# Normed input of four stages in buffers of its own, at 72, 68, 80 and 88 bytes past the weights' place

## Chip, cores and metric

The kernel runs on one core of a Trainium2 chip. The metric is the device time of one execution, in microseconds. The time before is 1128.12 us, the median of 3 runs (1127.64 to 1128.2).

## The reference

One sequence of 256 tokens with 1024 channels goes through a first block (a hybrid mixer with a state-space branch and three attention branches, and a gated feed-forward), and a second block of two layers: an HGRN2 mixer and a feed-forward, then a recurrent RG-LRU mixer and a feed-forward. All is float32. Cut to what the change touches:

```python
h = rmsnorm(x, norm_ffn[l])                     # first feed-forward
x = x + swiglu(h, w_ffn_gate[l], w_ffn_up[l], w_ffn_down[l])
...
for l in range(DEPTH_2):                        # second block, two layers
    hn = rmsnorm_2(x, norm_mix[l])
    if l % N_MIXERS == 0:
        mix = hgrn2_mixer(hn, ...)              # the "second mixer": hn @ w_in, w_in 1024 x 4096
    else:
        mix = rglru_mixer(hn, ...)              # the "third mixer"
    x = x + mix
    x = x + swiglu_2(rmsnorm_2(x, norm_ffn[l]), ffn_w_in[l], ffn_w_out[l])

def swiglu_2(h, w_in, w_out):
    gate, up = jnp.split(h @ w_in, [D_FF_2], axis=-1)   # D_FF_2 = 2816
    return (jax.nn.silu(gate) * up) @ w_out
```

## The kernel before

The normed input `h` is held transposed, channels on the 128 partitions, as 8 slices of 256 tokens. Each float32 value is split in two numbers of the type float32r, a high and a low part: `hh` and `hl` for the input, `whi` and `wlo` for the weights. A product of input and weights is then three: whi with hh, wlo with hh, whi with hl.

Weights come in units of at most 2048 elements per partition (1 MB) into a ring of three slots: `raw` by DMA, `whi` by ScalarE's copy (L1041), `wlo` by VectorE's or GpSimd's subtraction (L1465, L2143). The order of units is one list. All engines follow it, and each program is written out in order, with semaphores between engines.

TensorE has two forms of product. In `still` (L521, L524, L529) a 128 x 128 piece of the weights is loaded and the input moves, 256 columns at a time; gate and up units of a feed-forward and the column units of the mixers use it. A unit of 256 weight columns is 2 column blocks by 8 slices by 3 products, 48 matmuls, in groups of four slices. In `moving` (L541, L545, L549) a piece of the input is loaded and 512 columns of weights move; the token units (`hv`, `hg` of the second mixer) and the down and output products (`add_product`) use it.

The stages have a number e: 0 is the first mixer's input, 2 the first feed-forward, 3 the second mixer, 5 the second feed-forward, 6 the third mixer, 7 the third feed-forward. In each of them the normed rows `hn` are transposed on TensorE (L591), ScalarE copies the result into the high part (L1073) and VectorE subtracts for the low part (L1531). Each feed-forward has 11 gate and 11 up units, then 11 down units.

Every stage writes the same `hh` and `hl`. Their place matters for this change, so it is told in bytes of a partition. Buffers are laid out in the order in which they are written down, `raw` from 0. `whi` begins at 24,576 and `wlo` at 49,152; a slot is 8192 bytes and a piece of weights starts at a multiple of 512 bytes (in a unit of 256 columns). In this document "at n bytes" means n bytes past a multiple of 512, the weights' place:

| buffer | where it begins | at |
|---|---|---|
| hh, hl | 90,144 and 98,336 | 32 |
| eh, el (mixer outputs; share the space of hh, hl) | 90,112 and 98,304 | 0 |
| bh, bl (branch outputs, first mixer) | 133,696 and 141,888 | 64 |
| gh, gl (feed-forward's inner values) | 117,248 and 139,776 | 0 |
| gw (gate weights, third mixer) | 192,512 | 0 |

`sr`, 640 elements per feed-forward, is scratch in which GpSimd combines inner values for three of the down units (L2273 to L2277); ScalarE (L1284) and VectorE (L1888) round it.

Of the kernel before, what the change touches and what calls it, by code (L numbers as in the profile page):

```python
# [8 lines left out]
f32 = mybir.dt.float32  # L9
f32r = mybir.dt.float32r  # L10
# [11 lines left out]
SEVEN = (1, 4, 6)  # L22
# [53 lines left out]
def build(nc, a):  # L76
    V, A, G, T, S = nc.vector, nc.scalar, nc.gpsimd, nc.tensor, nc.sync
    vq, aq, gq, tq, sq = Waits(V), Waits(A), Waits(G), Waits(T), Waits(S)
    with ExitStack() as root:
# [3 lines left out]
        def sbuf(ctx, name, shape, dt=f32):  # L83
            return ctx.enter_context(nc.sbuf_tensor(name, shape, dt))
# [43 lines left out]
        dv = sbuf(mix, "dv", [128, 2, 128])  # L128
        mix.close()

        ffn = []
        for f in range(3):
            ctx = ExitStack()
            ffn.append((sbuf(ctx, f"gh_{f}", [128, 22, 256], f32r), sbuf(ctx, f"gl_{f}", [128, 22, 256], f32r),
                        sbuf(ctx, f"sg_{f}", [128, 2, 512]), sbuf(ctx, f"bc_f{f}", [128, 256]),
                        sbuf(ctx, f"sh_{f}", [128, len(SEVEN), 512], f32r), sbuf(ctx, f"sl_{f}", [128, len(SEVEN), 512], f32r),
                        sbuf(ctx, f"sr_{f}", [128, 640])))
            ctx.close()

        hg = ExitStack()  # L140
# [10 lines left out]
        nw = sbuf(hg, "nw", [128, 128])  # L151
        mstat = sbuf(hg, "mstat", [128, 16])
        bc_hg = sbuf(hg, "bc_hg", [128, 256])
        hg.close()

        lr = ExitStack()
# [8 lines left out]
        th = sbuf(lr, "th", [128, 8, 256])  # L165
        yg = sbuf(lr, "yg", [128, 8, 256])
        bc_lr = sbuf(lr, "bc_lr", [128, 256])
        gw = sbuf(lr, "gw", [128, 2, 4, 512])
        lr.close()

        def two(ap):
            return ap.rearrange("p (k t) -> p k t", k=2)
# [122 lines left out]
        NU = len(units)  # L295

        seven = {unit_at["down", f, n]: len(SEVEN) * f + i for f in range(3) for i, n in enumerate(SEVEN)}
        sums_raw, sums_hi, sums_lo = (t.rearrange("p (q n) -> p q n", n=512) for t in (
            hn_flat, eh[:, :, :].rearrange("p c t -> p (c t)"), el[:, :, :].rearrange("p c t -> p (c t)")))  # L300
# [86 lines left out]
        def bank_of(*key):  # L387
            return banks[turns[key][0]]
# [113 lines left out]
        def tensor_program():  # L502
# [49 lines left out]
            def of_norm(e):  # L552
                return (lambda k: hh_set(e, k)), (lambda k: hl_set(e, k))

            def project_columns(key, e, between=None):
                j = unit_at[key]
                b = turn(("col", *key), next_bank())
                tq.wait_ge(*free(("col", *key)))
                for m in range(units[j][2] // 128):
                    t = still(banks[b][:, 256 * m:256 * m + 256], j, m, hh, hl, range(8), *of_norm(e))  # L560
                    if between is not None and m == 0:
                        between()
                t.then_inc(s_full[b], 1)
                used[j, 0] = used[j, 1] = full("col", *key)

            def project_tokens(key, e, between=None):
                bs = [turn(("tok", *key, 0), next_bank()), turn(("tok", *key, 1), next_bank(), 2)]
                for part in range(2):
                    j = unit_at[(*key, part)]
                    for t in range(2):  # L570
                        if part == 0:
                            tq.wait_ge(*free(("tok", *key, t)))
                        tok = moving(banks[bs[t]][:, :], j, t, hh, hl, range(4 * part, 4 * part + 4), 0, 512, *of_norm(e),
                                     first=part == 0, last=part == 1)
                        if t == 1 or part == 1:
                            tok.then_inc(s_full[bs[t]], 1)
                    b, _, n = turns["tok", *key, 1]
                    used[j, 0] = used[j, 1] = (s_full[b], n - 1 + part)
                    if between is not None:
                        between(part)  # L580
# [21 lines left out]
            def project_pair(keys, e):  # L602
                js = [unit_at[key] for key in keys]
                bs = [turn(("col", *key), next_bank(), 2) for key in keys]
                for part in range(2):
                    for i, j in enumerate(js):
                        for m in range(2):
                            if part == 0:
                                tq.wait_ge(*free(("col", *keys[i])))
                            tok = still(banks[bs[i]][:, 256 * m:256 * m + 256], j, m, hh, hl, range(4 * part, 4 * part + 4),  # L610
                                        *of_norm(e), i0=4 * part, first=part == m == 0, last=part == m == 1,
                                        inside=(lambda: spread_factors(e)) if part == i == 1 and m == 0 and e == 3 else None)
                        tok.then_inc(s_full[bs[i]], 1)
                        used[j, part] = (s_full[bs[i]], turns["col", *keys[i]][2] - 1 + part)
                        if part == i == 0:
                            transposes(1, e)
                        if part == 1 and i == 0 and e != 3:
                            spread_factors(e)
# [411 lines left out]
        def scalar_program():  # L1030
# [38 lines left out]
            def turned(c, e):  # L1069
                for n in range(2):  # L1070
                    q = 2 * c + n
                    aq.wait_ge(*full("tr", e, q))
                    A.activation(hh[:, 2 * q:2 * q + 2, :], two(bank_of("tr", e, q)[:, :]), ACT.Copy).then_inc(s_hh, 1)  # L1073

            def project_pair(keys, e, bc, evacs):
                j = unit_at[keys[0]]
# [198 lines left out]
            add_product(("wo",), 4, 2)  # L1275

            def feed_forward(f, e, e2, again=None):
                gh, gl, sg, bc, sh, _, sr = ffn[f]

                def combined(j):  # L1280
                    if j in SEVEN:
# [169 lines left out]
        def vector_program():  # L1451
# [74 lines left out]
            def turned(c, e):  # L1526
                for n in range(2):
                    q = 2 * c + n
                    sl = slice(2 * q, 2 * q + 2)
                    vq.wait_ge(*hh_set(e, 2 * q))  # L1530
                    V.tensor_tensor(hl[:, sl, :], two(bank_of("tr", e, q)[:, :]), hh[:, sl, :].bitcast(f32),  # L1531
                                    ALU.subtract).then_inc(evacuated("tr", e, q), 1)

            def spread_factor(e):
# [344 lines left out]
            series = [None]  # L1879

            def feed_forward(f, e, e2, again=None):
                gh, gl, sg, bc, sh, sl, sr = ffn[f]

                def combined(j):
                    if j in SEVEN:
# [243 lines left out]
        def gpsimd_program():  # L2129
# [136 lines left out]

            def combine(f, j):

                q, inner, sr = seven[unit_at["down", f, j]], two(ffn[f][2][:, j % 2, :]), ffn[f][6]
                gq.wait_ge(*evac("col", "u", f, j))  # L2270
                if q > 0:
                    gq.wait_ge(s_comb_lo, q)
                d = own_p.mark(G.tensor_tensor(sr[:, 0:256], inner[:, 0, :], inner[:, 1, :], ALU.subtract))  # L2273
                G.tensor_tensor(sr[:, 384:512], inner[:, 0, 0:128], inner[:, 0, 128:256], ALU.subtract)
                gq.wait_ge(*d)
                G.tensor_tensor(sr[:, 256:384], sr[:, 128:256], inner[:, 0, 0:128], ALU.subtract)
                G.tensor_tensor(sr[:, 512:640], sr[:, 128:256], sr[:, 0:128], ALU.subtract).then_inc(s_comb, 1)  # L2277
# [144 lines left out]
```

## Time and profile before

| what | us |
|---|---|
| median of 3 runs | 1128.12 |
| the profiled execution | 1127.9 |
| its span, first to last instruction | 1126.6 |
| TensorE busy (matmuls) | 1111.4 |
| TensorE busy (weight loads) | 1034.5 |
| VectorE busy | 757.1 |
| ScalarE busy | 589.2 |
| GpSimd busy | 249.3 |

The granted clock of TensorE was 0.999 of the full 2.4 GHz over the span. PE is TensorE's matmul, PEld its weight load, DVE VectorE, ACT ScalarE, POOL GpSimd. Matmuls overlap, so a mean duration in a row is longer than the distance between two starts. In the timeline, like instructions that follow one another are merged into one row; its time is the start of the first of them. The names behind the arrow are the moving operand and then the loaded one: `hh,whi` is the input moving over loaded weights, `whi,hh` the weights moving over loaded input.

### The profile page before, as it was taken

How to read it: one execution, taken by the hardware profiler on the slowest of the kernel's cores; microseconds unless marked ns; L12 is line 12 of the kernel's file. 1: busy time of each engine (PE TensorE's matmuls, PEld its weight loads, DVE VectorE, ACT ScalarE, POOL GpSimd, SP SyncE). 2: the span in 40 equal slices, each digit the busy share in tenths (PEclk: the TensorE clock that was granted, in tenths of full speed). 3: DMA queues.
4: the chain of work that ended last, by engine and by line, in shares of the span. 5: the costliest groups of instructions: out<-in, count | busy, mean ns of one | idle time of the engine just before them, and what ended most of it. 6: DMA issues, size and time to landing. Idle time of an engine off the chain costs nothing.

```text
span 1126.6 us, 19386 instructions
## 1 busy us (share of the span) xinstructions
PE 1111.4 (99%) x8058; PEld 1034.5 (92%) x8058; DVE 757.1 (67%) x1160; ACT 589.2 (52%) x893; POOL 249.3 (22%) x202
## 2 busy tenths in 40 slices
PE   8999999999999999999999999999999999999997
PEld 7899989999989999888998889999889989999986
DVE  6755655677777456968897576444868896544676
ACT  6645555555545554536642554444536855444542
POOL 3022100000005554001411206553000003555100
PEclk9999999999999999999999999999999999999999
DMA  8689475544646756664545447656655355666561
GB/s 277 196 253 336 137 234 157 157 151 148 199 160 203 206 160 215 209 202 127 170 129 172 128 149 258 219 182 201 207 187 178 104 170 159 214 189 189 170 220 38
DMA packets 155090, 207.26 MB, mean 184 GB/s; under 512 B 9472, under 2 KB 128410, under 8 KB 155003
## 3 DMA queue, kind: packets, MB, share of 16 engines
q1 hardware_dynamic: 151274, 193.11, 54.6%
q0 software_dynamic: 3728, 12.92, 3.5%
q8 instruction: 64, 1.05, 0.4%
q14 instruction: 24, 0.19, 0.1%
HBM read 204.78 MB, written 4.24 MB: 186 GB/s over the span
## 4 chain that ended last, share of the span: by engine, by line
PE 81%; DVE 13%; ACT 4%; issue 2%; DMA 0%; POOL 0%; SPq 0%; DVEq 0%; ACTq 0%
PE bank L521 16%; PE bank L524 16%; PE bank L529 16%; PE bank L549 7%; PE bank L545 7%; PE bank L541 7%; DVE wlo L1465 4%; PE bank L660 1%; PE bank L656 1%; PE bank L659 1%; PE bank L946 1%; ACT whi L1041 1%; PE bank L860 1%; PE bank L870 1%; DVE area L1659 1%
## 5 line engine op out<-in xcount | busy, mean ns | idle before, releaser
L1465 DVE TENSOR_TENSOR wlo<-raw,whi 128x1024 fp32r<-128x1024 f32 x302 | 360.5, 1226 | 148.1 <-ACT whi L1041 147.1
L1041 ACT ACTIVATE whi<-raw 128x1024 fp32r<-128x1024 f32 (+1 forms) x362 | 356.5, 1034 | 80.5 <-PE bank L549 52.2
L521 PE MATMUL bank<-hh,whi 128*128 128x256 f32 x1784 | 284.6, 281 | 0.3 <-ACT hh L1073 0.3
L529 PE MATMUL bank<-hl,whi 128*128 128x256 f32 x1784 | 281.7, 279 | 0.4 <-DVE hl L1531 0.3
L524 PE MATMUL bank<-hh,wlo 128*128 128x256 f32 x1784 | 281.3, 279 | 0.0
L521 PEld LDWEIGHTS bank<-hh,whi 128*128 128x128 f32 x1784 | 240.7, 188 | 2.8 <-issue 2.0
L529 PEld LDWEIGHTS bank<-hl,whi 128*128 128x128 f32 x1784 | 239.9, 188 | 0.8 <-DVE hl L1531 0.8
L524 PEld LDWEIGHTS bank<-hh,wlo 128*128 128x128 f32 x1784 | 239.8, 188 | 0.0
L2143 POOL TENSOR_TENSOR wlo<-raw,whi 128x1024 fp32r<-128x1024 f32 x60 | 153.4, 2557 | 143.2 <-ACT whi L1041 143.1
L2150 POOL TENSOR_TENSOR st<-st,half 128x1 f32<-128x1 f32 x18 | 10.8, 607 | 476.1 <-DVE st L1524 442.1
L1288 ACT ACTIVATE sg<-sg 128x512 f32<-128x512 f32 x33 | 20.9, 633 | 96.4 <-DVE sg L1554 96.4
L1292 ACT ACTIVATE gh<-sg 128x512 fp32r<-128x512 f32 x33 | 20.8, 632 | 78.4 <-DVE sg L1901 78.4
L541 PE MATMUL bank<-whi,gh 128*128 128x512 f32 x192 | 59.3, 390 | 0.0
L545 PE MATMUL bank<-wlo,gh 128*128 128x512 f32 x192 | 59.2, 389 | 0.0
L549 PE MATMUL bank<-whi,gl 128*128 128x512 f32 x192 | 59.2, 389 | 0.0
L1901 DVE TENSOR_TENSOR sg<-sg,bank 128x512 f32<-128x512 f32 x33 | 22.7, 687 | 42.8 <-PE bank L529 40.7
L1554 DVE TENSOR_TENSOR sg<-bank,bc_f 128x512 f32<-128x512 f32 x33 | 22.7, 689 | 38.7 <-PE bank L529 38.7
L1066 ACT ACTIVATE bank<-x_sb 128x512 f32<-128x512 f32 x26 | 15.6, 600 | 61.9 <-DVE x_sb L1580 34.1
L1903 DVE TENSOR_TENSOR gl<-sg,gh 128x512 fp32r<-128x512 f32 x33 | 31.5, 956 | 23.3 <-ACT gh L1292 23.3
L549 PEld LDWEIGHTS bank<-whi,gl 128*128 128x128 f32 x192 | 36.0, 188 | 7.6
L545 PEld LDWEIGHTS bank<-wlo,gh 128*128 128x128 f32 x192 | 36.0, 188 | 7.5
L541 PEld LDWEIGHTS bank<-whi,gh 128*128 128x128 f32 x192 | 35.7, 188 | 7.1
(363 smaller groups left out, 1454.2 us busy)
## 6 DMA issues: line engine op xcount, KB each, us to landing
raw<-in_ffn_w_in SPq DMA_DIRECT2D x88, 512.0 KB, 3.8
raw<-in_w_in SPq DMA_DIRECT2D x72, 512.0 KB, 4.7
raw<-in_ffn_w_out SPq DMA_DIRECT2D x44, 512.0 KB, 3.6
raw<-in_hgrn_w_in SPq DMA_DIRECT2D x32, 512.0 KB, 4.3
raw<-in_w_ffn_gate SPq DMA_DIRECT2D x22, 512.0 KB, 4.6
raw<-in_w_ffn_up SPq DMA_DIRECT2D x22, 512.0 KB, 4.3
raw<-in_w_ffn_down SPq DMA_DIRECT2D x22, 512.0 KB, 3.9
raw<-in_w_branch SPq DMA_DIRECT2D x16, 512.0 KB, 4.5
```

The costliest lines, as they stand in the source:

```text
L521: T.matmul(out, wh[:, i, c], xh[:, k, :], start=first and (i, k) == pairs[0], stop=False)
L524: T.matmul(out, wl[:, i, c], xh[:, k, :], start=False, stop=False)
L529: t = T.matmul(out, wh[:, i, c], xl[:, k, :], start=False, stop=last and (i, k) == pairs[-1])
L541: tok = T.matmul(out, xh[:, k, r], wh[:, i, c], start=first and i == 0, stop=False)
L545: tok = T.matmul(out, xh[:, k, r], wl[:, i, c], start=False, stop=False)
L549: tok = T.matmul(out, xl[:, k, r], wh[:, i, c], start=False, stop=last and i == len(ks) - 1)
L1041: A.activation(split_of(whi, j, h), split_of(raw, j, h), ACT.Copy).then_inc(s_hi[j % NS][h], 1)
L1465: V.tensor_tensor(split_of(wlo, j, h), split_of(raw, j, h), split_of(whi, j, h).bitcast(f32), ALU.subtract).then_inc(s_lo[j % NS][h], 1)
L1554: V.tensor_tensor(dst, two(bank_of("col", *key)[:, :]), bc[:, :].rearrange("p (o t) -> p o t", o=1).broadcast_to([128, 2, 256]), ALU.mult) ...
L1901: V.tensor_tensor(s, s, bank_of("col", "u", f, j)[:, :], ALU.mult).then_inc(evacuated("col", "u", f, j), 1)
L1903: V.tensor_tensor(gl[:, 2 * j:2 * j + 2, :], two(s), gh[:, 2 * j:2 * j + 2, :].bitcast(f32), ALU.subtract).then_inc(s_gl, 1)
L2143: G.tensor_tensor(half_of(wlo, j, 1), half_of(raw, j, 1), half_of(whi, j, 1).bitcast(f32), ALU.subtract).then_inc(s_lo[j % NS][1], 1)
```

## The change

Four stages get a normed input of their own, one buffer each of 4096 + 32 elements, in which the high and the low part begin at a chosen byte: 72 past the weights' place for the first feed-forward (e = 2), 68 for the second mixer (e = 3), 80 for the second feed-forward (e = 5), 88 for the third (e = 7). The first and third mixer (e = 0 and 6) keep `hh` and `hl` at 32 bytes. To make room, `sr` becomes a view of `hn`, and unused gaps keep the new buffers off the space that is loaded ahead for the next mixer; `gw` moves by 3,712 bytes.

The new buffers begin at 190,976 (first feed-forward, second mixer) and 179,712 (second and third feed-forward), both multiples of 512. The high part lies at the chosen byte behind that and the low part 8192 bytes further.

On each of the five queues the instructions, their shapes and their waits stand in the same order as before. Only operands differ.

```diff
@@ -128,13 +128,15 @@
         dv = sbuf(mix, "dv", [128, 2, 128])
         mix.close()
 
-        ffn = []
+        ffn, normed_ffn = [], []
         for f in range(3):
             ctx = ExitStack()
             ffn.append((sbuf(ctx, f"gh_{f}", [128, 22, 256], f32r), sbuf(ctx, f"gl_{f}", [128, 22, 256], f32r),
                         sbuf(ctx, f"sg_{f}", [128, 2, 512]), sbuf(ctx, f"bc_f{f}", [128, 256]),
-                        sbuf(ctx, f"sh_{f}", [128, len(SEVEN), 512], f32r), sbuf(ctx, f"sl_{f}", [128, len(SEVEN), 512], f32r),
-                        sbuf(ctx, f"sr_{f}", [128, 640])))
+                        sbuf(ctx, f"sh_{f}", [128, len(SEVEN), 512], f32r), sbuf(ctx, f"sl_{f}", [128, len(SEVEN), 512], f32r)))
+            if f == 0:
+                sbuf(ctx, "gap_levels", [128, 2816])
+            normed_ffn.append(sbuf(ctx, f"normed_{f}", [128, 4096 + 32], f32r))
             ctx.close()
 
         hg = ExitStack()
@@ -151,6 +153,8 @@
         nw = sbuf(hg, "nw", [128, 128])
         mstat = sbuf(hg, "mstat", [128, 16])
         bc_hg = sbuf(hg, "bc_hg", [128, 256])
+        sbuf(hg, "gap_normed", [128, 48])
+        normed_hg = sbuf(hg, "normed_hg", [128, 4096 + 32], f32r)
         hg.close()
 
         lr = ExitStack()
@@ -165,8 +169,15 @@
         th = sbuf(lr, "th", [128, 8, 256])
         yg = sbuf(lr, "yg", [128, 8, 256])
         bc_lr = sbuf(lr, "bc_lr", [128, 256])
+        sbuf(lr, "gap_gw", [128, 928])
         gw = sbuf(lr, "gw", [128, 2, 4, 512])
         lr.close()
+
+        def normed_at(t, byte):
+            return tuple(t[:, byte // 4 + 2048 * i:byte // 4 + 2048 * i + 2048].rearrange("p (k t) -> p k t", k=8) for i in range(2))
+
+        NORMED = {0: (hh, hl), 2: normed_at(normed_ffn[0], 72), 3: normed_at(normed_hg, 68), 5: normed_at(normed_ffn[1], 80),
+                  6: (hh, hl), 7: normed_at(normed_ffn[2], 88)}
 
         def two(ap):
             return ap.rearrange("p (k t) -> p k t", k=2)
@@ -295,6 +306,7 @@
         NU = len(units)
 
 
+        sr = hn[:, 1, 0:640]
         seven = {unit_at["down", f, n]: len(SEVEN) * f + i for f in range(3) for i, n in enumerate(SEVEN)}
         sums_raw, sums_hi, sums_lo = (t.rearrange("p (q n) -> p q n", n=512) for t in (
             hn_flat, eh[:, :, :].rearrange("p c t -> p (c t)"), el[:, :, :].rearrange("p c t -> p (c t)")))
@@ -557,7 +569,7 @@
                 b = turn(("col", *key), next_bank())
                 tq.wait_ge(*free(("col", *key)))
                 for m in range(units[j][2] // 128):
-                    t = still(banks[b][:, 256 * m:256 * m + 256], j, m, hh, hl, range(8), *of_norm(e))
+                    t = still(banks[b][:, 256 * m:256 * m + 256], j, m, *NORMED[e], range(8), *of_norm(e))
                     if between is not None and m == 0:
                         between()
                 t.then_inc(s_full[b], 1)
@@ -570,7 +582,7 @@
                     for t in range(2):
                         if part == 0:
                             tq.wait_ge(*free(("tok", *key, t)))
-                        tok = moving(banks[bs[t]][:, :], j, t, hh, hl, range(4 * part, 4 * part + 4), 0, 512, *of_norm(e),
+                        tok = moving(banks[bs[t]][:, :], j, t, *NORMED[e], range(4 * part, 4 * part + 4), 0, 512, *of_norm(e),
                                      first=part == 0, last=part == 1)
                         if t == 1 or part == 1:
                             tok.then_inc(s_full[bs[t]], 1)
@@ -607,7 +619,7 @@
                         for m in range(2):
                             if part == 0:
                                 tq.wait_ge(*free(("col", *keys[i])))
-                            tok = still(banks[bs[i]][:, 256 * m:256 * m + 256], j, m, hh, hl, range(4 * part, 4 * part + 4),
+                            tok = still(banks[bs[i]][:, 256 * m:256 * m + 256], j, m, *NORMED[e], range(4 * part, 4 * part + 4),
                                         *of_norm(e), i0=4 * part, first=part == m == 0, last=part == m == 1,
                                         inside=(lambda: spread_factors(e)) if part == i == 1 and m == 0 and e == 3 else None)
                         tok.then_inc(s_full[bs[i]], 1)
@@ -1070,7 +1082,7 @@
                 for n in range(2):
                     q = 2 * c + n
                     aq.wait_ge(*full("tr", e, q))
-                    A.activation(hh[:, 2 * q:2 * q + 2, :], two(bank_of("tr", e, q)[:, :]), ACT.Copy).then_inc(s_hh, 1)
+                    A.activation(NORMED[e][0][:, 2 * q:2 * q + 2, :], two(bank_of("tr", e, q)[:, :]), ACT.Copy).then_inc(s_hh, 1)
 
             def project_pair(keys, e, bc, evacs):
                 j = unit_at[keys[0]]
@@ -1275,7 +1287,7 @@
             add_product(("wo",), 4, 2)
 
             def feed_forward(f, e, e2, again=None):
-                gh, gl, sg, bc, sh, _, sr = ffn[f]
+                gh, gl, sg, bc, sh, _ = ffn[f]
 
                 def combined(j):
                     if j in SEVEN:
@@ -1528,7 +1540,7 @@
                     q = 2 * c + n
                     sl = slice(2 * q, 2 * q + 2)
                     vq.wait_ge(*hh_set(e, 2 * q))
-                    V.tensor_tensor(hl[:, sl, :], two(bank_of("tr", e, q)[:, :]), hh[:, sl, :].bitcast(f32),
+                    V.tensor_tensor(NORMED[e][1][:, sl, :], two(bank_of("tr", e, q)[:, :]), NORMED[e][0][:, sl, :].bitcast(f32),
                                     ALU.subtract).then_inc(evacuated("tr", e, q), 1)
 
             def spread_factor(e):
@@ -1879,7 +1891,7 @@
             series = [None]
 
             def feed_forward(f, e, e2, again=None):
-                gh, gl, sg, bc, sh, sl, sr = ffn[f]
+                gh, gl, sg, bc, sh, sl = ffn[f]
 
                 def combined(j):
                     if j in SEVEN:
@@ -2266,7 +2278,7 @@
 
             def combine(f, j):
 
-                q, inner, sr = seven[unit_at["down", f, j]], two(ffn[f][2][:, j % 2, :]), ffn[f][6]
+                q, inner = seven[unit_at["down", f, j]], two(ffn[f][2][:, j % 2, :])
                 gq.wait_ge(*evac("col", "u", f, j))
                 if q > 0:
                     gq.wait_ge(s_comb_lo, q)
```

## Rows read from the trace of the kernel before

**Rows 1.** Page, parts 1 and 5: busy us (share) xinstructions; costliest groups of TensorE.

```profile
PE 1111.4 (99%) x8058; PEld 1034.5 (92%) x8058; DVE 757.1 (67%) x1160; ACT 589.2 (52%) x893; POOL 249.3 (22%) x202
...
L521 PE MATMUL bank<-hh,whi 128*128 128x256 f32 x1784 | 284.6, 281 | 0.3 <-ACT hh L1073 0.3
L529 PE MATMUL bank<-hl,whi 128*128 128x256 f32 x1784 | 281.7, 279 | 0.4 <-DVE hl L1531 0.3
L524 PE MATMUL bank<-hh,wlo 128*128 128x256 f32 x1784 | 281.3, 279 | 0.0
```

**Rows 2.** Waits of TensorE: line waited for: us in total, times, longest.

```profile
PE bank L705 <- DMA wrow<-in_norm_mix: 2.2, 1, 2.2
PE bank L713 <- DVE hn L1622: 1.9, 1, 1.9
PE bank L545 <- DVE wlo L1465: 1.6, 3, 0.7
```

**Rows 3.** Windows: the three feed-forward projections behind their first units; columns in the first row.

```profile
core 0: us, PE busy (x) PEld busy (x) DVE busy (x) ACT busy (x) POOL busy (x), PEclk, DMA share, GB/s
342.16:457.04 114.88, 114.88 (x987) 114.88 (x986) 68.23 (x85) 61.39 (x74) 57.98 (x32) 1.00 0.65 195
678.64:793.53 114.89, 114.89 (x987) 114.89 (x986) 59.17 (x60) 54.58 (x67) 58.91 (x32) 1.00 0.67 212
947.72:1062.61 114.89, 114.89 (x987) 114.89 (x986) 59.19 (x60) 55.84 (x68) 58.91 (x32) 1.00 0.64 194
```

**Rows 4.** Timeline, TensorE, first feed-forward: start us, us, engine line op, xcount.

```profile
400.11 0.63 PE L524 MATMUL bank<-hh,wlo 128*128 128x256 f32 x4
400.58 0.63 PE L529 MATMUL bank<-hl,whi 128*128 128x256 f32 x4
...
411.31 0.63 PE L524 MATMUL bank<-hh,wlo 128*128 128x256 f32 x4
```

**Rows 5.** Timeline, TensorE, third mixer's column units.

```profile
907.83 0.63 PE L529 MATMUL bank<-hl,whi 128*128 128x256 f32 x4
...
912.07 0.63 PE L529 MATMUL bank<-hl,whi 128*128 128x256 f32 x4
```

**Rows 6.** Timeline, TensorE, a branch product of the first mixer.

```profile
301.89 0.39 PE L524 MATMUL bank<-bh,wlo 128*128 128x256 f32 x2
...
309.60 0.39 PE L529 MATMUL bank<-bl,whi 128*128 128x256 f32 x2
```

**Rows 7.** Timeline, TensorE, an earlier branch product.

```profile
225.80 0.40 PE L529 MATMUL bank<-bl,whi 128*128 128x256 f32 x2
...
230.04 0.40 PE L529 MATMUL bank<-bl,whi 128*128 128x256 f32 x2
```

**Rows 8.** Timeline, TensorE, a token unit of the second mixer.

```profile
596.13 1.10 PE L545 MATMUL bank<-wlo,hh 128*128 128x512 f32 x4
...
599.86 1.10 PE L549 MATMUL bank<-whi,hl 128*128 128x512 f32 x4
```

**Rows 9.** Timeline, TensorE, the first mixer's output product.

```profile
315.29 0.62 PE L541 MATMUL bank<-whi,eh 128*128 128x512 f32 x2
...
319.83 0.39 PE L545 MATMUL bank<-wlo,eh 128*128 128x512 f32 x1
```

**Rows 10.** Timeline, TensorE, 64 columns wide, second mixer.

```profile
591.62 3.68 PE L946 MATMUL bank<-qT,kT 128*128 128x64 f32 x32
595.11 1.18 PE L541 MATMUL bank<-whi,hh 128*128 128x512 f32 x4
```

**Rows 11.** Timeline, TensorE, first units of the second mixer.

```profile
516.29 0.89 PE L521 MATMUL bank<-hh,whi 128*128 128x256 f32 x4 [0.29 <-ACT hh L1073]
...
517.95 1.10 PE L529 MATMUL bank<-hl,whi 128*128 128x256 f32 x4 [0.31 <-DVE hl L1531]
...
528.80 0.71 PE L599 MATMUL bank<-ident,diag 128*128 128x128 f32 x4 [0.21 <-DVE diag L1537]
```

**Rows 12.** Timeline, TensorE, gates of the third mixer.

```profile
876.01 14.08 PE L1012 MATMUL bank<-uc,gw 128*128 128x256 f32 x64
889.74 0.47 PE L521 MATMUL bank<-hh,whi 128*128 128x256 f32 x1
```

## The prediction

> **What bounds the kernel now.** I began with the page: in its first part TensorE is busy for 1111.4 of 1126.6 us and its weight loads for 1034.5, while VectorE has 757.1 [rows 1]. The three costliest TensorE groups are the products of the normed input with the weights' two parts, 1784 each. The list of waits on TensorE comes next. Its longest entries are 2.2, 1.9 and 1.6 us, and everything listed adds up to some 9 us [rows 2]. So TensorE waits for nobody for any length. Only its own rate is left to look at, and the table of windows says that inside a feed-forward's projection it has no idle time at all: 114.88 of 114.88 us, with VectorE at 59 to 68, ScalarE at 55 to 61, GpSimd at 58 to 59, and the DMA share at 0.64 to 0.67, at granted clock 1.00 [rows 3].
>
> A row's mean of 280 ns is no price here, since matmuls overlap. What counts is the step from one start to the next, and that is read from the timeline: first start to last start, divided by the matmuls between.
> - Feed-forward projection, moving operand hh or hl at 32 bytes: L524 at 400.11 to L524 at 411.31, 24 groups of four, 11.20 / 96 = 116.7 ns [rows 4].
> - The same code and the same place in the third mixer: L529 at 907.83 to L529 at 912.07, 36 matmuls in 4.24 us, 117.8 ns [rows 5].
> - Branch product, moving operand bh or bl at 64 bytes: L524 at 301.89 to L529 at 309.60, 34 groups of two, 7.71 / 68 = 113.4 ns [rows 6].
> - The same branch product, same place, earlier: 225.80 to 230.04, 36 matmuls in 4.24 us, 117.8 ns [rows 7].
> - The 512-wide form with the input as the loaded operand: hh at 32 bytes, 596.13 to 599.86, 16 matmuls, 233.1 ns [rows 8]; eh at 0 bytes, 315.29 to 319.83, 20 matmuls, 227.0 ns [rows 9].
>
> All of these have every operand ready and the clock at full. Two things follow. Where the two operands lie relative to one another goes along with a difference of 3 to 6 ns a step. And one place has more than one steady step: bh holds 113.4 in one stretch and 117.8 in another, hh 116.7 and 117.8. 
>
> **The change part by part.** Instructions: none is added or removed, and each engine's queue has the same instructions, shapes and waits in the same order; only names differ. So no wait can arise from a new order, and no DMA is issued earlier or later by the program.
>
> *The three feed-forwards.* Each has 22 gate and up units of 2 column blocks by 8 slices by 3 products, 1056 matmuls, so 3168. They go from 32 bytes to 72, 80 and 88. No row of this trace has an operand at such a place; the nearest is bh at 64. From below: the step can't be expected under the weight load's own one. The nearest row for that is L946, only 64 wide, whose 32 matmuls take 3.49 us, 109.1 ns each [rows 10]. That gives 3168 x 7.6 = 24.1 us of gain. From above: the slow rhythm, 117.8 ns, gives a loss of 3168 x 1.1 = 3.5 us, and the farthest row, what 32 bytes cost the wide form (6.1 ns), laid on top of 116.7 would be 19.3 us. I take the nearest row, 113.4 ns. These runs are long and nothing stands between their matmuls, as in the stretch where bh held 113.4. Gain 3168 x 3.3 = 10.5 us.
>
> *The second mixer's column units.* hf and hq are 8 units, 384 matmuls, from 32 to 68 bytes. The first pair of units waits for VectorE and ScalarE at its start (idle of 0.29 and 0.31 us, and 0.21 for the spread factors) [rows 11], so a faster step there is taken back. That is 96 of them. The other 288 at 3.3 ns give 0.9 us, between 2.2 (at 109.1 ns) and a loss of 0.3.
>
> *The second mixer's token units.* hv and hg are 4 keys by 2 parts by 2 token blocks by 12, 192 matmuls 512 wide with the normed input as the loaded operand. From 233.1 to the 227.0 that eh has is 192 x 6.1 = 1.2 us. From above, one more such penalty is a loss of 1.2. I take the gain.
>
> *What costs nothing.* ScalarE's copy into the input's high half and VectorE's subtraction into the low half write the same 512 elements per partition and are the same count; if each took 0.1 us longer, 16 on the path would be 1.6 us, but nothing in the rows says that a write's place matters. The scratch of the combined activations moves into hn: GpSimd's and VectorE's steps on it keep their shapes, and GpSimd is busy for half of a projection, which hides them [rows 3]. The gate weights gw move too, from a multiple of 512 to 128 past one. Their 64 matmuls take 13.73 us together [rows 12], 215 ns each, and at 3 ns either way this is 0.2 us. Also nothing.
>
> *What is late next.* A unit of 48 matmuls shrinks from 5.60 to 5.44 us. In that time VectorE, ScalarE and GpSimd have their 48 to 59% of work, and the weights' transfers their share of 0.67, so 3% more speed leaves each well under 0.7. I see no wait that would take it back, apart from the edges already subtracted.
>
> The sum: 10.5 + 0.9 + 1.2 = 12.6 us. The profiled execution took 1127.9 us (span 1126.6), and the median of the runs is 1128.12, 0.2 above. Forecast 1128.1 - 12.6 = 1115.5 us.
>
> On the places of operands the Trainium skill says the opposite. "SBUF — State Buffer", section "SBUF: two separate sides", says that only the port shared by VectorE and GpSimd causes contention, and that TensorE never waits on anyone; "TensorE: Matmul & The Clock Gate", section "Step-by-step: what each phase is for", gives TensorE two independent read ports, so that loading the next weights takes no read bandwidth from the running matmul. By that the change is worth nothing and the time stays at 1128. Rows 4 and 6 disagree with it, at 116.7 against 113.4 ns for the same shape. The same page's section "Back-to-back issue gap" has N / 2.4 + 2.5 ns for an isolated gap, an estimate of 109.2 ns at 256 columns; by it the feed-forwards would gain 3168 x 7.5 = 24 us.
>
> **The rivals.**
> - *The place does not decide.* The state at a stretch's start would choose the step, as it does between rows 4 and 5 and between rows 6 and 7. For it: two steps at one place. Against it: 113.4 never shows with hh at 32 bytes in the projections I followed, and all three projections take 114.88 or 114.89 us. This is also what the skill's port rule comes to. Time 1128.1.
> - *The slow rhythm.* The new places fall into the rhythm of rows 5 and 7, 117.8 ns, for the whole of each projection. For it: bh at 64, the nearest place, held it too, and 72 to 88 bytes were never seen. Against it: it showed in short stretches behind other work. It decides once over three quarters of the 3168 take it, since 2376 x 1.1 = 2.6 us is what the other 792 gain at 3.3; at all of them +3.5, and +0.4 for the mixer, 1132.0 us. This is the case on the slower side.
> - *Half of it.* One or two projections fall into 113.4 and the rest stay, or every rhythm comes to about 115: half of the sum, 6.3 us, 1121.8 us.
> - *Below the nearest row.* A place that is no multiple of 32 frees the streams altogether, 109.1 ns: 24.1 + 2.2 + 1.2 = 27.5 us, 1100.6; something between, at 111.5 ns, gives 18 us and 1110. Against it: with 0, 32 and 64 bytes alike, no 256-wide row is under 113.
>
> **How the numbers follow.** Forecast 0.52; half 0.18; no effect 0.09; slow rhythm 0.14; below 0.07. The likeliest one alone spans 1112 to 1119. To leave out no more than 2 in 10, the range goes from 1110, which takes in the upper part of the last case, to 1128.5, which takes in no effect but not the slow rhythm. A run of this kernel tells a difference of 0.2%, 2.3 us, from none. Faster by more: 0.52 + 0.18 + 0.07 = 0.77. Within: 0.09. Slower: 0.14.
>
> **What would show it.** In the timeline of the changed kernel, groups of four in each feed-forward's projection should start 0.453 us apart and not 0.467, and the stretch from the spread factors to the first down product should last 111.6 us and not 114.9. Token units of the second mixer should go in steps of 227 ns. First and third mixer and the down products should keep their steps. I am wrong if the groups stay 0.467 apart (the place does not decide), if they are 0.471 apart (slow rhythm), if the three projections differ, or if they are faster but VectorE or a landing weight shows up in TensorE's list of waits with over 2 us.

## The result, and the profile after

The changed kernel takes 1138.92 us (median of 4 runs, 1138.77 to 1139.42) against 1128.16: ratio 1.0097, interval 1.0085 to 1.0109. It is 10.8 us slower. Forecast were 1115.5 us and a range that ended at 1128.5.

The profiled execution took 1138.85 us, with a span of 1137.6. The page's part 1 and its costliest group of matmuls in the changed kernel, which answer to [rows 1]:

```profile
PE 1122.7 (99%) x8058; PEld 1046.2 (92%) x8058; DVE 753.9 (66%) x1160; ACT 589.1 (52%) x893; POOL 251.2 (22%) x202
...
L533 PE MATMUL bank<-normed,whi 128*128 128x256 f32 x1056 | 170.0, 283 | 0.0
```

TensorE has as many instructions as before and is busy 11.3 us longer; the span is 11.0 longer. VectorE and ScalarE have no more work than before, GpSimd 1.9 us more. TensorE's longest waits in the changed kernel, the answer to [rows 2], have hardly moved either:

```profile
PE bank L717 <- DMA wrow<-in_norm_mix: 2.3, 1, 2.3
PE bank L725 <- DVE hn L1634: 1.8, 1, 1.8
PE bank L557 <- DVE wlo L1477: 1.6, 3, 0.7
```

The windows over the three projections, from the first matmul behind the spread factors to the first down product, answer to [rows 3]:

```profile
342.38:460.55 118.17, 118.17 (x988) 118.17 (x987) 65.77 (x85) 61.37 (x74) 58.34 (x32) 1.00 0.64 189
682.79:800.96 118.17, 118.17 (x988) 118.17 (x987) 58.55 (x60) 54.53 (x67) 58.08 (x32) 1.00 0.65 206
955.41:1073.55 118.14, 118.14 (x987) 118.14 (x986) 58.56 (x60) 55.81 (x68) 58.08 (x32) 1.00 0.61 189
```

Each is 3.3 us longer at clock 1.00, and no other engine has over 0.4 us more work in it. That is 9.8 of the 11.0 us. The timeline of TensorE in the first of them gives the step, against [rows 4]:

```profile
400.55 0.64 PE L536 MATMUL bank<-normed,wlo 128*128 128x256 f32 x4
...
411.11 0.64 PE L541 MATMUL bank<-normed,whi 128*128 128x256 f32 x4
```

22 groups of four in 10.56 us are 120.0 ns a matmul, where it was 116.7. The three places 72, 80 and 88 all have this step. In the second mixer's column units, at 68 bytes, the timeline shows:

```profile
541.04 0.65 PE L536 MATMUL bank<-normed_hg,wlo 128*128 128x256 f32 x4
...
545.87 0.65 PE L541 MATMUL bank<-normed_hg,whi 128*128 128x256 f32 x4
```

10 groups in 4.83 us, 120.8 ns; this stage's columns cost 1.1 us more (60.7 us from 519.76 to 580.45, 59.6 before). Five of the eight token units keep their 233 ns, as in [rows 8], and three have 231.4 to 231.7, a gain of about 0.1 us. Some 0.6 us come back in the token part of the stage, where TensorE waited 0.2 us for VectorE's `Ss` before and no longer does; the rest of the 0.6 was not traced. From its first column unit to its output product the second mixer takes 129.8 us, and 129.3 before. So the 11.0 us are 9.8 in the projections, 0.7 in the feed-forwards' first units (72 matmuls each, ahead of the window) and 0.5 in the second mixer.

### The profile page after: what moved, and what is told of

It reads as the page before. It is cut to its first block, busy times and chain, and to the rows that moved or that the text cites. A ratio compares the mean times of both kernels' runs of the same rounds, so it can differ in the third digit from the quotient of the medians.

```text
span 1137.6 us, 19386 instructions
## 1 busy us (share of the span) xinstructions
PE 1122.7 (99%) x8058; PEld 1046.2 (92%) x8058; DVE 753.9 (66%) x1160; ACT 589.1 (52%) x893; POOL 251.2 (22%) x202
## 4 chain that ended last, share of the span: by engine, by line
PE 86%; DVE 8%; ACT 3%; issue 1%; DMA 0%; SPq 0%; POOL 0%; DVEq 0%; ACTq 0%
PE bank L533 18%; PE bank L536 18%; PE bank L541 18%; PE bank L561 7%; PE bank L557 7%; PE bank L553 7%; DVE wlo L1477 3%; PE bank L958 2%; PE bank L672 1%; PE bank L671 1%; PE bank L668 1%; ACT whi L1053 1%; PE bank L872 1%; PE bank L882 1%; PE bank L603 1%
## 5 line engine op out<-in xcount | busy, mean ns | idle before, releaser
L533 PE MATMUL bank<-normed,whi 128*128 128x256 f32 x1056 | 170.0, 283 | 0.0
L541 PE MATMUL bank<-normed,whi 128*128 128x256 f32 x1056 | 169.5, 282 | 0.0
L536 PE MATMUL bank<-normed,wlo 128*128 128x256 f32 x1056 | 169.5, 282 | 0.0
L533 PEld LDWEIGHTS bank<-normed,whi 128*128 128x128 f32 x1056 | 145.6, 190 | 0.2
L541 PEld LDWEIGHTS bank<-normed,whi 128*128 128x128 f32 x1056 | 145.5, 190 | 0.0
L536 PEld LDWEIGHTS bank<-normed,wlo 128*128 128x128 f32 x1056 | 145.5, 190 | 0.0
L533 PE MATMUL bank<-hh,whi 128*128 128x256 f32 x600 | 96.6, 283 | 0.0
L536 PE MATMUL bank<-hh,wlo 128*128 128x256 f32 x600 | 94.7, 279 | 0.0
L541 PE MATMUL bank<-hl,whi 128*128 128x256 f32 x600 | 94.6, 279 | 0.0
L533 PEld LDWEIGHTS bank<-hh,whi 128*128 128x128 f32 x600 | 81.1, 188 | 1.8 <-issue 1.4
L536 PEld LDWEIGHTS bank<-hh,wlo 128*128 128x128 f32 x600 | 80.8, 188 | 0.0
L541 PEld LDWEIGHTS bank<-hl,whi 128*128 128x128 f32 x600 | 80.8, 188 | 0.0
```

The source lines that it names most:

```text
L533: T.matmul(out, wh[:, i, c], xh[:, k, :], start=first and (i, k) == pairs[0], stop=False)
L536: T.matmul(out, wl[:, i, c], xh[:, k, :], start=False, stop=False)
L541: t = T.matmul(out, wh[:, i, c], xl[:, k, :], start=False, stop=last and (i, k) == pairs[-1])
```

## The experiments

All compare with the kernel before, run beside each: medians of 1127.6 to 1128.3 us. Where no interval is given, the kernel was run once. The places of the buffers in each kernel were taken from its built program. There buffers begin at multiples of 32 bytes, which matters for three of the edits below. A "step" is a start-to-start distance within a stretch.

**1. Own buffers, but all at 32 bytes.**

```diff
-        NORMED = {..., 2: normed_at(normed_ffn[0], 72), 3: normed_at(normed_hg, 68), 5: normed_at(normed_ffn[1], 80),
+        NORMED = {..., 2: normed_at(normed_ffn[0], 32), 3: normed_at(normed_hg, 32), 5: normed_at(normed_ffn[1], 32),
-                  6: (hh, hl), 7: normed_at(normed_ffn[2], 88)}
+                  6: (hh, hl), 7: normed_at(normed_ffn[2], 32)}
```

> All four stages keep the buffers of their own, with sr in hn and gw moved, but every input lies at 32 bytes past the weights' place, as hh did before. Theory A (the place relative to the weights sets the step): the three feed-forward projections step by 116.7 ns again, 480 ns per group of four become 467, time 1128.1 +- 1 us. Theory B (the buffers' region, sr or gw cost it, or the place chosen has nothing to do with it): the steps stay at 120.0 ns and the time at 1138 to 1139 us.

Measured 1128.16 us, ratio 1.0001 (0.9992 to 1.0011). The windows over its projections:

```profile
342.42:457.30 114.88, 114.88 (x987) 114.88 (x986) 68.23 (x85) 61.38 (x74) 57.95 (x32) 1.00 0.65 194
678.84:793.73 114.89, 114.89 (x987) 114.89 (x987) 59.18 (x60) 54.55 (x67) 58.95 (x32) 1.00 0.67 212
```

These are the lengths of [rows 3] to 0.01 us. New buffers, `sr` in `hn` and the moved `gw` cost nothing together. The whole loss is the choice of bytes.

**2. Other places, one for each stage** (the same edit, with 0, 64, 64 and 96).

> First feed-forward at 0 bytes, second mixer and second feed-forward at 64, third feed-forward at 96. The three projections are the same code and had one step in common in both kernels (116.7 and 120.0), so each is a test of one place. Theory A with the reading of the prediction: 64 gives 113.4 ns in the second feed-forward (groups of four 0.453 us apart) and about 227 ns in the mixer's token units; 0 and 96 unknown, between 113 and 120. Rival (the step depends on the form of the unit, and the branch product's 113.4 says nothing on a feed-forward): 64 gives 117 to 120 in the second feed-forward.

Measured 1136.41 us. Windows over the projections at 0, 64 and 96 bytes:

```profile
342.80:461.00 118.20, 118.20 (x988) 118.20 (x987) 65.85 (x85) 61.36 (x74) 58.66 (x32) 1.00 0.64 189
682.60:798.60 116.00, 116.00 (x987) 116.00 (x987) 59.06 (x60) 54.55 (x67) 58.88 (x32) 1.00 0.67 210
953.00:1071.20 118.20, 118.20 (x987) 118.20 (x987) 58.58 (x60) 55.80 (x68) 58.05 (x32) 1.00 0.62 189
```

At 64 bytes, the place from which the prediction took its 113.4 ns, a feed-forward has 116.0 us / 984 = 117.9 ns. The rival's number came true. The mixer's token units at 64 stayed at 233 ns, where the theory had 227.

**3. Everything moved together.** The kernel before, and below it the changed kernel, with a gap ahead of the weights:

```diff
         raw = sbuf(root, "raw", [128, NS, UC])
+        sbuf(root, "gap_all", [128, 2])        # in the changed kernel: 14
         whi = sbuf(root, "whi", [128, NS, UC], f32r)
```

> The kernel before with one gap of 8 bytes ahead of the weights' buffers, so all buffers but raw begin 8 bytes later: relative places as before, absolute places no multiple of 32. Theory A (relative place): nothing changes, 1128.1 +- 1 us, steps 116.7 and 227. Theory C (an operand that starts off a multiple of 32 or 64 bytes costs by itself, which 68, 72, 80 and 88 all do): every product gets slower, 120 ns instead of 116.7 in the projections, 1138 us or more.

> The changed kernel with one gap of 56 bytes ahead of the weights' buffers: relative places 72, 68, 80, 88 as changed; absolute places 128, 124, 136, 144 past a multiple of 512, so that the first feed-forward's input starts at a multiple of 128 bytes and the weights at 56. Theory A: all three projections stay at 120.0 ns, 1138.9 us. Theory C, if the moving operand's start counts: the first feed-forward falls to 116.7 or lower and the others stay.

Measured 1128.22 us (ratio 1.000, 0.999 to 1.0009) and 1139.40 us, with all projections as long as without the gap. Because buffers begin at multiples of 32, the gaps moved everything by 32 and by 64 bytes, not by 8 and 56. So the runs don't test an operand start off a multiple of 32. They do show that a common move of 32 or 64 bytes changes nothing. The sweep below disposes of the alignment theory in another way: 0, 64 and 96 are multiples of 32 and slow, and 112, which is none, is the fastest.

**4. The weights moved alone.** The kernel before with `whi` and `wlo` 32 bytes further and hh where it was:

```diff
         raw = sbuf(root, "raw", [128, NS, UC])
+        sbuf(root, "gap_all", [128, 8])
...
-        sbuf(root, "gap_hh", [128, 8])
```

> The kernel before with the weights' buffers 32 bytes further and everything from hh on where it was (the gap ahead of hh is gone). The moving operand reads the same addresses as before; only the place of the loaded weights changes, and hh now lies at 0 bytes from theirs. Theory (the moving read and the weight load of the next matmul clash): the projections go at 120.0 ns, as with an input of its own at 0, although hh has not moved; 3168 x 3.3 = 10.6 us and the mixers' share on top, 1138 to 1145 us. Rival (the moving operand's own address sets the step): 116.7 ns, no change in the projections.

Measured 1146.24 us. The timeline of its first feed-forward, and below it of a token unit:

```profile
400.27 0.64 PE L529 MATMUL bank<-hl,whi 128*128 128x256 f32 x4
...
411.31 0.64 PE L524 MATMUL bank<-hh,wlo 128*128 128x256 f32 x4
...
604.46 1.08 PE L545 MATMUL bank<-wlo,hh 128*128 128x512 f32 x4
...
608.11 1.08 PE L549 MATMUL bank<-whi,hl 128*128 128x512 f32 x4
```

23 groups in 11.04 us: 120.0 ns, the step of an own buffer at 0 bytes, though hh stands where it stood for 116.7. So the moving operand's own address does not set the step; its place relative to the weights does. The run's time lies above the expected 1138 to 1145, and it is not the price of hh alone: bh, gh and gw stood still too and so changed their places relative to the weights. The three projections lose 9.8 us, the first mixer 3.1, and the down products 4.5, their steps going from 227 to about 233 ns. The token form goes from 233 to 228 ns with the same edit. The two forms want different places: at 0 bytes one has its best step seen and the other a bad one. The Trainium skill ("TensorE: Matmul & The Clock Gate", section "Step-by-step: what each phase is for") says that weights load through a port of their own, without taking bandwidth from the running matmul. Experiments 3 and 4 side by side are hard to square with two reads that leave each other alone: moving the weights alone costs 3.3 ns a matmul, and moving both operands together costs nothing. They don't show what the two reads share.

**5. The sweep** (the edit of 1 with other numbers; for 136 and 160 bytes the first feed-forward's buffer is 32 elements longer).

> Places: first feed-forward 16 bytes, second mixer 48, second feed-forward 40, third 48. Seen so far in the projections: 0 gives 120.0 ns, 32 gives 116.7, 64 gives 117.8, 72 to 96 give 120.0. Theory (a good place is narrow and lies around 32): 40 and 48 lie between 116.7 and 117.8 or at 113 to 115, 16 at 116.7 to 120. Rival (any step off 32 costs): all three over 116.7.

> Places: first feed-forward 24 bytes, second mixer 16, second feed-forward 56, third 8. Theory: steps change little from one place to the next, so 24 is near 32 (116.7), 56 near 64 (117.8), 8 near 0 (120.0). If some place gives 113.3 ns, which the branch product has shown, it is in this sweep.

> Places: first feed-forward 160 bytes, second mixer 40, second feed-forward 36, third 112. If the pattern repeats every 128 bytes, 160 acts as 32 and gives 116.7 ns, and 112 lies between 96 and 128, which is 0, at 120.0. If it repeats over more than that, 160 gives another step. 36 tells whether 4 bytes off the best place matter: 116.7 or slightly over.

> Places around the best: first feed-forward 136 bytes, second mixer 96, second feed-forward 104, third 120. If 112 sits in a wide valley, 104 and 120 are at 113.3 to 116; if it is one narrow place (as 32 is between 24 at 120.0 and 36 at 121.7), both are at 117 to 122. 136 would be at 120.0 if the pattern had a period of 128 bytes (8 gave 120.0), which 160 at 117.3 against 32 at 116.7 already speaks against.

> Places: first feed-forward and second mixer 128 bytes, second feed-forward 108, third 116. If the run with hh shared was at 128 as reckoned, the first feed-forward steps by 118.7 ns as there. If 112 is one narrow place, 108 and 116 are at 118 to 122 (104 gave 120.0, 120 gave 121.1); if the valley is 16 bytes wide, one of them at 113 to 116.

Measured 1134.94, 1136.45, 1131.32, 1140.91 and 1141.13 us. The third of these runs has 160, 36 and 112 bytes in its three windows:

```profile
342.90:458.44 115.54, 115.54 (x988) 115.54 (x987) 68.23 (x85) 61.41 (x74) 57.85 (x32) 1.00 0.65 193
680.70:800.50 119.80, 119.80 (x988) 119.80 (x987) 58.37 (x60) 54.54 (x67) 57.88 (x32) 1.00 0.65 204
954.40:1066.01 111.61, 111.61 (x987) 111.61 (x986) 61.80 (x60) 55.97 (x68) 59.12 (x32) 1.00 0.64 200
```

Length of a projection's 984 matmuls, by place, in us:

| place | us | place | us | place | us |
|---|---|---|---|---|---|
| 0 | 118.2 | 48 | 116.5 | 108 | 118.2 |
| 8 | 118.2 | 56 | 116.5 | **112** | **111.6** |
| 16 | 116.9 | 64 | 116.0 | 116 | 120.6 |
| 24 | 118.2 | 72, 80, 88 | 118.2 | 120 | 119.3 |
| **32** | **114.9** | 96 | 118.2 | 128 | 118.2 |
| 36 | 119.8 | 104 | 118.2 | 136, 160 | 118.2, 115.5 |
| 40 | 118.2 | | | | |

Most entries are one stage in one profile, and 128 bytes gave 118.2 us here and 116.8 in another layout (experiment 7), so differences under 1.4 us say little about a place.

Steps don't change little by little. Four bytes to either side of 112 cost 6.6 and 9.0 us a projection; four bytes behind 32 cost 4.9. The theory of a valley fell: 24 is as 0 and not as 32. The rival of the first of these runs, that any place off 32 costs, held for its three. A period of 128 bytes is not settled. 128 came out as 0 and 136 as 8, but 118.2 is also what most places have, and 160 differs from 32 by only 0.6 us. Places beyond 160 were not tried.

**6. High and low part at different places** (high 72, low 32; 32 and 64 in the second mixer; 32 and 72; 32 and 64).

> High and low part at different places: first feed-forward high 72, low 32; second mixer high 32, low 64; second feed-forward high 32, low 72; third high 32, low 64. Theory local (each matmul's step follows its own operand's place): in the first feed-forward two thirds of the matmuls at 120.0 and one third at 116.7, mean 118.9; second 117.8; third 117.0. Theory global (the stream as a whole falls into one rhythm): groups of all three products have the same length in each projection, whichever part moves, and the mean need not lie between.

Measured 1132.87 us; the projections take 117.35, 117.05 and 114.87 us. Timeline of the third, low part at 64 (L542), high at 32:

```profile
1010.20 0.64 PE L534 MATMUL bank<-normed,whi 128*128 128x256 f32 x4
1010.68 0.63 PE L537 MATMUL bank<-normed,wlo 128*128 128x256 f32 x4
1011.15 0.62 PE L542 MATMUL bank<-normed,whi 128*128 128x256 f32 x4
1011.60 0.64 PE L534 MATMUL bank<-normed,whi 128*128 128x256 f32 x4
```

Groups of 0.48, 0.47 and 0.45 us. They are not equal, so "global" in its plain form fell. But the low part at 64 has 0.45 us here, where a stretch wholly at 64 has 0.47, and the second projection comes to 119.0 ns a matmul (117.05 / 984) where "local" said 117.8 (the first has 119.3 for 118.9, the third 116.7 for 117.0). A group's length depends on its neighbours too. Neither theory holds.

**7. Everything at 112.** First the four inputs of their own:

> All four inputs of their own at 112 bytes, the place that gave 113.3 ns in one projection. Theory (the place sets the step of a long projection, in all three alike): 3168 x 3.3 = 10.6 us less than before, and up to 1.3 for the second mixer's column units if they take 113.3 too: 1116.5 to 1118 us. Rival (113.3 was the state in which that one stretch happened to start, as the branch product shows two steps at one place): at least one of the three projections has another step, 1120 to 1128 us.

Measured 1117.69 us, ratio 0.9908 (0.9893 to 0.9923). Timeline of its first feed-forward:

```profile
399.98 0.61 PE L536 MATMUL bank<-normed,wlo 128*128 128x256 f32 x4
...
411.31 0.61 PE L541 MATMUL bank<-normed,whi 128*128 128x256 f32 x4
```

25 groups in 11.33 us, 113.3 ns, and all three projections take 111.62 us. The theory's number held. The second mixer gained nothing: its columns take 0.6 us less, and TensorE then waits 0.9 us for VectorE's `Ss`, where it waited 0.2 before. Beside it went a simpler edit, the kernel before with a wider gap:

```diff
-        sbuf(root, "gap_hh", [128, 8])
+        sbuf(root, "gap_hh", [128, 28])
...
-        sbuf(root, "gap_stage", [128, 80])
+        sbuf(root, "gap_stage", [128, 60])
```

> The kernel before with no buffers of its own: hh and hl lie at 112 bytes instead of 32 (a gap of 28 elements for 8), for all six stages. Theory: the projections go at 113.3 ns, as in the run beside it, and the first and third mixer's column units, some 1850 matmuls at 116.6 to 117.8 before, gain 3 to 4 ns each as far as they fall into the same rhythm: 1110 to 1117 us. Rival (short stretches between other work do not settle, or 112 is worse there, as the branch product at 64 shows two steps): the mixers stay or lose a little, 1117 to 1120 us.

Measured 1143.07 us, ratio 1.0133 (1.0117 to 1.015). The text on record is wrong about its place: with buffers at multiples of 32, hh stood at 128, bh at 96 and gh at 32. Its projections take 116.8 us, against 118.2 with an own buffer at 128: one place, two steps, in the same form of unit. In the run of the sweep with 128, the second mixer's column units had 118.7 ns at that place and the first feed-forward 120.1, in buffers that begin at the same byte. Then the mixers' shared input at 112, as a slice:

```diff
-        sbuf(root, "gap_hh", [128, 8])
-        hh = sbuf(root, "hh", [128, 8, 256], f32r)
-        hl = sbuf(root, "hl", [128, 8, 256], f32r)
+        normed_mix = sbuf(root, "normed_mix", [128, 4096 + 32], f32r)
+        hh, hl = (normed_mix[:, 28 + 2048 * i:28 + 2048 * i + 2048].rearrange("p (k t) -> p k t", k=8) for i in range(2))
```

> The kernel with the four inputs of their own at 112 bytes (1117.7 us), and the shared input of the first and third mixer at 112 too, as a slice of one buffer, so that the place is really reached: buffers begin at multiples of 32 bytes, so the earlier run with a gap of 28 elements had hh at 128 bytes, the branch inputs at 96 and the inner values at 32. Theory (112 gives 113.3 to 113.8 ns in column units of any stage): about 1850 matmuls gain 3 to 4 ns, 5.5 to 7.5 us, 1110 to 1112.5 us. Rival (short stretches between other work keep their old steps of 116.6 to 117.8): 1117 to 1118 us.

Measured 1113.92 us, ratio 0.9875 (0.9859 to 0.9891). Timeline of the third mixer's column units, against [rows 5]:

```profile
882.07 0.61 PE L532 MATMUL bank<-normed_mix,whi 128*128 128x256 f32 x4
...
895.21 0.61 PE L540 MATMUL bank<-normed_mix,whi 128*128 128x256 f32 x4
```

29 groups in 13.14 us: 113.3 ns, from 117.8. Short stretches take the step too, but most of them late: behind a pause the first 7 to 15 steps take up to 123 ns, and only then does 113.3 hold. The gain beyond the kernel with four is 3.8 us and not the 5.5 to 7.5 expected, and 3.7 of it lie in the first mixer. In the third, a wait takes the gain back. It is listed below as it was before and as it is in this kernel:

```profile
PE bank L541 <- DVE cl L2084: 0.6, 1, 0.6
...
PE bank L552 <- DVE cl L2095: 1.4, 1, 1.4
```

From its first column unit to its output product the third mixer takes 60.9 us, 61.1 before. Another part of the difference is the branch product, which lies where it lay and now runs at 117.8 throughout, also where it ran at 113.4 before. Last, that product's inputs at 112 (the same kind of slice, 12 elements into a buffer that begins at 64 bytes):

> The kernel with all six normed inputs at 112 bytes (1113.9 us), and the branch product's inputs bh and bl moved from 64 to 112 too. The prediction carried a step from the branch product to the column units of a feed-forward and failed; this asks the other way round. Theory (a good place is good for one form only, since the branch units' weights lie in rows of 2048 bytes and the column units' in rows of 1024): no gain to be counted on, branch products anywhere from 113.3 to 120 ns, time between 1113 and 1115 us. Rival (112 is good for every product with the input moving): 113.3 ns instead of 117.8 in 384 matmuls, 1.7 us, 1112.2 us.

Measured 1112.74 us, ratio 0.9862 (0.9846 to 0.9879), the fastest kernel here. Timeline, against [rows 6]:

```profile
294.41 0.39 PE L532 MATMUL bank<-branches,whi 128*128 128x256 f32 x2
...
299.85 0.39 PE L532 MATMUL bank<-branches,whi 128*128 128x256 f32 x2
```

24 groups of two in 5.44 us, 113.3 ns. The theory written down there, that a good place is good for one form only, fell for 112 among the products in which the input moves. The gain was 1.2 us of the rival's 1.7.

## Why the prediction was wrong, point by point

- **TensorE's step alone decides: right.** 9.8 of 11.0 us lie in the projections, and no wait listed for TensorE grew by more than 0.2 us. Nothing was added, removed or reordered, and experiment 1 shows the by-products at nothing (forecast: nothing).
- **The step that failed: "I take the nearest row, 113.4 ns".** The term 3168 x 3.3 = 10.5 us of gain came out as a loss of about the same size, at 120.0 ns. Two choices were wrong in it. Nearness in bytes carries no information here: the sweep changes by up to 9 us a projection within 4 bytes. And the row was the faster of two that the same place showed ([rows 6] and [rows 7]), from another form of unit. It does not even belong to its place: among the 13 profiles, before included, whose kernels have all relative places alike up to that product's end, it steps by 113.4 ns in six and by 117.8 in seven. Even at 64 bytes a feed-forward has 117.9 ns. The step that came, groups 0.480 us apart, was not among the signs that the prediction listed.
- **The slower side was bounded too low.** 117.8 ns stood as the slow rhythm, 1132 us, and the far bound of 19.3 us was named and not used. The trace of before held the right row, a column unit of the first mixer with hh at 32 bytes, and I had not read it:

```profile
199.88 0.64 PE L521 MATMUL bank<-hh,whi 128*128 128x256 f32 x4
...
205.16 0.64 PE L529 MATMUL bank<-hl,whi 128*128 128x256 f32 x4
```

  11 groups in 5.28 us are 120.0 ns. With it as the slow rhythm the rival's price is 3168 x 3.3 = 10.5 us, 1138.6, and the measured time is 1138.9. Its chance of 0.14 was too small as well: of 21 other places tried in projections, only 112 beats 32.
- **The second mixer.** Columns: forecast a gain of 0.9, measured a loss of 1.1, for the same reason; a shorter wait gave some 0.6 of it back. Tokens: forecast a gain of 1.2, measured about 0.1 from their step; 233 ns came at 64 and 112, 231 to 233 at 68, and 228 at 0.
- **"I see no wait that would take it back": not put to the test here, and wrong where it was.** This kernel has no faster step. In those with 112 bytes the projections kept their whole gain, but TensorE's wait for VectorE's `Ss` grew from 0.2 to 0.9 us in the second mixer and that for `cl` from 0.6 to 1.4 in the third.
- **"The place does not decide": wrong, but not wholly.** 128 bytes gave 118.2 and 116.8 us, and 16 gave 118.8 ns in a feed-forward and 116.7 in the second mixer. The step can switch with no place changed at all. [rows 5] have 117.8 ns, and the same column units in the kernel of experiment 3 whose relative places are all as before show:

```profile
907.50 0.63 PE L525 MATMUL bank<-hh,wlo 128*128 128x256 f32 x4
...
912.17 0.63 PE L530 MATMUL bank<-hl,whi 128*128 128x256 f32 x4
```

  10 groups in 4.67 us are 116.7 ns. So the state at a stretch's start has a say, and it is not the same in every profile; what it consists of stays open. At 112 every stretch of 24 or more column units' matmuls settled at 113.3 ns.
- **The size was right for another kernel.** At 112 bytes the projections reach the 113.4 and the 111.6 us that the prediction named as its sign. Nothing in the prediction pointed to that place; the sweep found it.

## What to carry to other kernels

Where a matmul stream has no idle time, read its start-to-start step in every stretch and list all the steps that one shape shows; the slowest of them is the least to put down for a bad place, and a step from another place, however near, is no estimate of a new one. A place of operands can't be reasoned out from neighbours: measure it, with one stage per candidate where a kernel has several alike, and read back the addresses of the built program, since a gap may be rounded. Then read the waits behind the short stretches: there a faster step can end in a longer wait.

## What the runs showed of the hardware

- With all operands ready at full clock, the 128 x 256 products of this kernel step by 113.3 to 122.6 ns, depending on where the moving operand lies relative to the loaded one. One place gave up to two steps: between layouts (118.7 and 120.1 at 128 bytes), and between profiles with all relative places alike (116.7 and 117.8 at 32; 113.4 and 117.8 for the branch product at 64).
- A common move of input and weights by 32 or 64 bytes changed no projection; moving the weights alone by 32 took the step from 116.7 to 120.0 ns.
- The best place for an input that moves over weights, 112 bytes past a multiple of 512, held in all six stages and in the branch product; 4 bytes behind it is the worst place seen (116: 120.6 us a projection), 4 bytes ahead of it is as slow as most (108: 118.2 us).
- The 512-wide form, in which the input is loaded, did not follow: 233 ns at 32, 64 and 112 bytes, 227 to 228 at 0.
